# Out-projection of a stream step as three products of high and low parts

## What is computed

```
h   = modulate(x, shift_m, scale_m)                         # adaLN
mix = W_out [ RetentionGroup(h) | StickBreakingGroup(h) ]   # the out-projection, 1024 x 1024
x   = layer_norm(alpha * x + gate_m * mix, ln_mix_g, ln_mix_b)
h   = modulate(x, shift_f, scale_f)
x   = layer_norm(alpha * x + gate_f * HierMoE(h))           # 16 experts, top 2 of one group
```

## Time and profile before

| | us |
|---|---|
| median of 3 launches | 1542.14 |
| lowest, highest | 1540.63, 1542.35 |
| the profiled launch | 1539.93 |
| span of its instructions | 1538.1 |
| mean granted TensorE clock, share of full | 0.947 |

### The profile page before, as it was taken

The page is one execution under the profiler, slowest core; times in us unless marked ns, Lnnn a source line. Parts: engine busy times, 40 slices in busy tenths (PEclk is TensorE's granted clock), DMA queues, the critical chain, the costliest instruction groups (busy, mean ns, idle before and its releaser), DMA issues.

```text
span 1538.1 us, 18365 instructions
## 1 busy us (share of the span) xinstructions
PE 1344.9 (87%) x6487; PEld 890.7 (58%) x6488; DVE 851.6 (55%) x1111; ACT 569.3 (37%) x751; POOL 334.8 (22%) x466
## 2 busy tenths in 40 slices
PE   5989999999899989999979992799999999999900
PEld 1433334466777856656535542588777788787700
DVE  5486875034531056576334556555888551528868
ACT  0200000123222156777422124145777442527632
POOL 0122310000420046676423341100000000000063
PEclk9999999999999999999989995799999999999955
DMA  9614131101121152121312615565899752529863
GB/s 345 242 55 164 55 118 54 55 1 31 38 69 41 49 179 55 29 56 29 138 55 96 246 62 205 194 229 218 311 384 388 281 184 89 218 75 381 315 231 131
DMA packets 138756, 234.44 MB, mean 152 GB/s; under 512 B 57320, under 2 KB 58928, under 8 KB 138696
## 3 DMA queue, kind: packets, MB, share of 16 engines
q1 hardware_dynamic: 128424, 196.39, 36.1%
q0 software_dynamic: 6496, 23.60, 4.5%
q10 hardware_dynamic: 3776, 13.67, 2.2%
HBM read 197.95 MB, written 35.68 MB: 152 GB/s over the span
## 4 chain that ended last, share of the span: by engine, by line
PE 60%; DVE 15%; issue 11%; ACT 5%; POOL 4%; DMA 2%; SPq 1%; ACTq 1%; POOLq 0%; DVEq 0%
PE psum L784 55%; DVE arena L1592 4%; POOL arena L1914 3%; PE psum L967 2%; ACT high L1376 2%; PE psum L1161 1%; DMA arena<-in_w_ada_mix 1%; DVE arena L1855 1%; DVE arena L1854 1%; DVE arena L1847 1%; DVE arena L1845 1%; DVE arena L1846 1%; DVE win_low L1572 1%; DVE arena L1593 1%; ACT a_high L1404 1%
## 5 line engine op out<-in xcount | busy, mean ns | idle before, releaser
L784 PE MATMUL psum<-arena 128*64 128x128 f32 (+7 forms) x1524 | 256.8, 365 | 11.6 <-DVE arena L1785 10.1
L784 PEld LDWEIGHTS psum<-arena 128*64 128x64 f32 (+3 forms) x1524 | 131.3, 157 | 117.2 <-issue 95.9
L784 PE MATMUL psum<-win,hT 128*128 128x512 f32 (+1 forms) x432 | 191.4, 597 | 0.5 <-ACT hT L1205 0.5
L784 PE MATMUL psum<-high,h_high 128*128 128x512 f32 x416 | 165.1, 397 | 2.5 <-DVE h_low L1801 2.5
L784 PE MATMUL psum<-high,h_low 128*128 128x512 f32 x416 | 163.2, 392 | 0.0
L784 PEld LDWEIGHTS psum<-win,hT 128*128 128x128 f32 (+1 forms) x432 | 77.6, 184 | 109.7 <-issue 105.5
L1659 DVE TENSOR_TENSOR_SCAN arena<-arena,psum 128x512 f32<-128x512 f32 (+4 forms) x116 | 109.5, 978 | 19.6 <-ACT arena L1329 19.5
L1796 DVE TENSOR_TENSOR low_odd<-raw_odd,high 128x2048 fp32r<-128x2048 f32 x48 | 107.8, 2289 | 13.9 <-ACT high L1376 13.9
L1796 DVE TENSOR_TENSOR low_even<-raw_even,high 128x2048 fp32r<-128x2048 f32 x48 | 107.7, 2287 | 10.8 <-ACT high L1376 10.8
L1914 POOL TENSOR_TENSOR arena<-arena 128x512 f32<-128x512 f32 (+4 forms) x116 | 108.2, 933 | 9.4 <-POOL arena L1911 0.2
L1958 POOL COPY smalls<-smalls 128x1 int32 x26 | 4.7, 182 | 421.6 <-PE psum L1161 415.9
(11 more groups left out here) (227 smaller groups left out, 2168.0 us busy)
## 6 DMA issues: line engine op xcount, KB each, us to landing
raw_even<-in_w_e_gate SPq DMA_DIRECT2D x8, 2048.0 KB, 10.6
raw_even<-in_w_e_up SPq DMA_DIRECT2D x8, 2048.0 KB, 16.4
raw_even<-in_w_e_down SPq DMA_DIRECT2D x8, 2048.0 KB, 14.7
raw_odd<-in_w_e_gate SPq DMA_DIRECT2D x8, 2048.0 KB, 10.1
raw_odd<-in_w_e_up SPq DMA_DIRECT2D x8, 2048.0 KB, 16.5
raw_odd<-in_w_e_down SPq DMA_DIRECT2D x8, 2048.0 KB, 14.7
win<-in_w_in SPq DMA_DIRECT2D x7, 2048.0 KB, 8.7
expert_rows<-arena ACTq DMA_DIRECT2D x26, 512.0 KB, 6.7
```

Of the source, the lines that this page charges most:

```text
L784: pe_last[0] = nc.tensor.matmul(*x, **y)
```

## The change

`wout` and the mixed input are split into high and low parts, and each product of the out-projection becomes three (`split_products`). The eight chunks of each half of `wout` are split piece by piece (`first_splits`): ACT writes `wout_high` (half 0 into the region of the queries, half 1 into that of the cache), DVE writes `wout_low` in place over `wout`. The first pieces lie in steps NG to NG+4 of the attention, between its last operations. Each tile's mixed rows are split too: ACT writes `mix_high` (128 x 1024, two buffers), DVE writes the low part in place. PE's early products of tile 0 inside the attention go; tile 0 is computed like the others, its first use of each chunk waiting for that piece. In ACT's loop the high part of tile t+1 stands between the two `copy_ret`; in DVE's loop the low part of tile t+1 stands first. `take_scales(*LATE)` moves behind tile 0's second half on DVE, `head_sums(*LATE)` behind half 0 of tile 0 on PE. Since `win_high` and `wout_high` lie where the first expert's weights go, SP issues that load in the last iteration, after all products, ahead of the last tile's stores.

```diff
@@ -198,8 +198,8 @@
 
         projected_f = named([("hT", r_a, KC * TOK), ("win", r_w, 8192)], F32)
-        projected_s = named([("x_low", r_a, KC * TOK), ("win_low", r_w, 8192), ("win_high", r_m, 9 * D),
-                             ("x_high", r_b + 8960, KC * TOK)], F32R)
+        projected_s = named([("mix_high", r_tmp, 2 * KC * P), ("x_low", r_a, KC * TOK), ("win_low", r_w, 8192),
+                             ("win_high", r_m, 9 * D), ("wout_high", r_sq, KC * 512), ("x_high", r_b + 8960, KC * TOK)], F32R)
         cst = view(r_const, C_MAIN)
         rot = view(r_sq, C_END - C_MAIN)
         ident = cst[:, C_IDENT:C_IDENT + 128]
@@ -252,7 +252,7 @@
         mixed = view(r_m, 9, D)
         hT, x_low, x_high = [t[:].rearrange("p (k n) -> p k n", k=KC)
                              for t in (projected_f["hT"], projected_s["x_low"], projected_s["x_high"])]
-        mixT = view(r_a, KC, TOK)
+        mixT = hT
         ada_b = [view(r_b + 4096 * i, KC, 512) for i in range(4)]
         ada_m = [view(r_m + 4096 * i, KC, 512) for i in range(2)]
         ada_rows = view(r_sq + C_END - C_MAIN, 2048)
@@ -262,7 +262,10 @@
         win, win_low = [[t[:, 4096 * i:4096 * i + 4096].rearrange("p (k n) -> p k n", k=KC) for i in range(2)]
                         for t in (projected_f["win"], projected_s["win_low"])]
         win_high = projected_s["win_high"][:].rearrange("p (k n) -> p k n", k=9)[:, 0:KC, 512:1024]
-        wout = view(r_w, KC, D)
+        wout_f = projected_f["win"][:].rearrange("p (k n) -> p k n", k=KC)
+        wout_low = projected_s["win_low"][:].rearrange("p (k n) -> p k n", k=KC)
+        wout_high = [projected_s["wout_high"][:].rearrange("p (k n) -> p k n", k=KC), win_high]
+        mix_high = projected_s["mix_high"][:].rearrange("p (i k q) -> p i k q", i=2, k=KC)
 
         qhT = view(r_b, 4, TOK)
@@ -395,9 +398,10 @@
             for name, table_at in (("cache", cache_at), ("sums", sums_at), ("scales", scales_at)):
                 if s in table_at:
                     enter((name,) + table_at[s], by_dve)
-        enter(("sums",) + LATE, by_dve)
         for t in range(1, TILES):
             enter(("ret", t), by_act, (7,))
+            if t == 1:
+                enter(("sums",) + LATE, by_dve)
             if t == 3:
                 enter(("scales",) + LATE, by_dve)
 
@@ -463,6 +467,23 @@
                         ret_i += 1
         N_TURN = turn_no
         assert N_TURN == 27
+
+        out_split_no = {}
+        for hh in range(2):
+            for k in range(KC):
+                if (hh, k) == (0, 4):
+                    out_split_no["mixed", 0] = len(split_no) + len(out_split_no) + 1
+                out_split_no["wout", hh, k] = len(split_no) + len(out_split_no) + 1
+        for t in range(1, TILES):
+            out_split_no["mixed", t] = len(split_no) + len(out_split_no) + 1
+        first_splits = {NG: [("wout", 0, 0), ("wout", 0, 1), ("wout", 0, 2)],
+                        NG + 1: [("wout", 0, 3), ("mixed", 0), ("wout", 0, 4), ("wout", 0, 5)],
+                        NG + 2: [("wout", 0, 6), ("wout", 0, 7), ("wout", 1, 0)],
+                        NG + 3: [("wout", 1, 1), ("wout", 1, 2), ("wout", 1, 3)],
+                        NG + 4: [("wout", 1, 4), ("wout", 1, 5), ("wout", 1, 6), ("wout", 1, 7)]}
+
+        def tile_cols(t):
+            return slice(t * P, t * P + rows_of(t))
 
         def ada_src(j):
             w = w_ada_mix if j < 6 else w_ada_ffn
@@ -684,7 +705,7 @@
                             "(t p) d -> p t d", p=P)).then_inc(s_kc[1], 16)
 
             load_cache(0)
-            sp.dma_start(wout, w_out[0].rearrange("(k p) n -> p k n", p=P)).then_inc(s_wout, 16)
+            sp.dma_start(wout_f, w_out[0].rearrange("(k p) n -> p k n", p=P)).then_inc(s_wout, 16)
             for pair in range(1, PAIRS):
                 load_cache(pair)
 
@@ -727,11 +748,10 @@
             for t in range(TILES):
                 if t + 2 < TILES:
                     load_x(t + 2)
-                if t == 3:
-                    sp.wait_ge(s_wt, ring_no["ret", LAST])
+                if t == LAST:
+                    sp.wait_ge(s_op, TILES)
                     load_expert(0, 0)
                 store_5(t)
-            sp.wait_ge(s_op, TILES)
             load_expert(1, 1)
             sp.wait_ge(s_lg, 9)
             sp.wait_ge(s_x1o[0], 16 * 5)
@@ -1034,9 +1054,12 @@
 
             def out_part(t, hh, ks):
                 r = rows_of(t)
+                cols = slice(hh * 512, (hh + 1) * 512)
                 for k in ks:
-                    last = mm(psum[t % 2][0:r, hh, :], mixT[:, k, t * P:t * P + r],
-                              wout[:, k, hh * 512:(hh + 1) * 512], start=(k == 0), stop=(k == KC - 1))
+                    if t == 0:
+                        pe.wait_ge(s_pL, out_split_no["wout", hh, k])
+                    last = split_products(psum[t % 2][0:r, hh, :], mix_high[:, t % 2, k, 0:r], x_low[:, k, tile_cols(t)],
+                                          wout_high[hh][:, k, :], wout_low[:, k, cols], k == 0, k == KC - 1)
                 return last
 
             pe.wait_ge(s_mr, 9)
@@ -1057,13 +1080,6 @@
                     head_sums(*sums_at[s])
                 if s in scales_at:
                     head_scales(*scales_at[s])
-                if s == NG + 1:
-                    wait_copied(pe, ("ret", 0))
-                    wait_copied(pe, ("scales", 2, 2))
-                    pe.wait_ge(s_wout, 16)
-                    out_part(0, 0, range(7))
-            out_part(0, 1, range(7))
-            head_sums(*LATE)
 
             def h2_turned(t):
                 r = rows_of(t)
@@ -1088,15 +1104,13 @@
             for t in range(TILES):
                 if t >= 2:
                     pe.wait_ge(s_ope, t - 1)
-                for piece, (t0, _, _) in enumerate(pieces):
-                    if t == t0:
-                        wait_copied(pe, ("scales", PAIRS - 1, piece))
-                if t:
-                    wait_copied(pe, ("ret", t))
+                pe.wait_ge(s_pL, out_split_no["mixed", t])
                 for hh in range(2):
                     if hh == 0 and 2 * t + 1 < TILES:
                         ret_turn(2 * t + 1)
-                    last = out_part(t, hh, range(KC) if t else (7,))
+                    last = out_part(t, hh, range(KC))
+                    if (t, hh) == (0, 0):
+                        head_sums(*LATE)
                     if (t, hh) == (1, 0):
                         head_scales(*LATE)
                     if hh == 0 and 2 * t + 2 < TILES:
@@ -1308,6 +1322,26 @@
                     last = A(mixT[:, k, t * P:t * P + r], bank(7)[:, k * P:k * P + r], ACT.Copy, scale=colv[:, 64 + k:65 + k])
                 last.then_inc(s_wte, 1)
 
+            def out_high(kind, *at):
+
+                if kind == "wout":
+                    hh, k = at
+                    if k == 0:
+                        act.wait_ge(s_wout, 16)
+                        act.wait_ge(s_pv if hh else s_qk, NG)
+                    A(wout_high[hh][:, k, :], wout_f[:, k, hh * 512:(hh + 1) * 512], ACT.Copy).then_inc(s_pH, 1)
+                else:
+                    t, = at
+                    if t >= 2:
+                        act.wait_ge(s_op, t - 1)
+                    else:
+                        act.wait_ge(s_qk, NG)
+                    act.wait_ge(s_wte, by_act["ret", t])
+                    for piece, (t0, t1_, _) in enumerate(pieces):
+                        if t0 <= t < t1_:
+                            wait_copied(act, ("scales", PAIRS - 1, piece))
+                    A(mix_high[:, t % 2, :, 0:rows_of(t)], hT[:, :, tile_cols(t)], ACT.Copy).then_inc(s_pH, 1)
+
             def square(pair, piece):
 
                 cols = piece_cols(piece)
@@ -1336,11 +1370,18 @@
                     copy_ret(0)
                 if s in squares_at:
                     square(*squares_at[s])
+                for split_ in first_splits.get(s, ()):
+                    out_high(*split_)
             square(*LATE)
+            for split_ in first_splits[NG + 4]:
+                out_high(*split_)
             for t in range(TILES + 2):
-                for v in (2 * t + 1, 2 * t + 2):
-                    if v < TILES:
-                        copy_ret(v)
+                if 2 * t + 1 < TILES:
+                    copy_ret(2 * t + 1)
+                if t + 1 < TILES:
+                    out_high("mixed", t + 1)
+                if 2 * t + 2 < TILES:
+                    copy_ret(2 * t + 2)
                 v = t - 1
                 if 0 <= v < TILES:
                     r = rows_of(v)
@@ -1616,6 +1657,18 @@
 
             step(V.tensor_copy(bank(7)[:, 0:1], ones_col))
 
+            def out_low(kind, *at):
+
+                dve.wait_ge(s_pH, out_split_no[(kind,) + at])
+                if kind == "wout":
+                    hh, k = at
+                    cols = slice(hh * 512, (hh + 1) * 512)
```

(15 more changed lines are left out.)

## The result

The changed kernel takes 1528.52 us (median of 4 launches, 1527.12 to 1530.7); the kernel before takes 1541.39 (median of 4). The ratio is 0.9936, 95% interval 0.9917 to 0.9955: faster by 12.9 us. The direction was forecast; the gain is 12.9 us instead of the 27.4 of the sum, and the time lies 0.5 us above the range.

The account below looks back on a forecast made before the run. PE was taken to bound the out-projection stage from tile 3 on. R(8) 25.4 us earlier plus 2.0 in the tail made 27.4 off the profiled 1539.93, as a median 1515 us; range 1506 to 1528.

Parts of the forecast that it names:

- PE's work: Out-projection on PE: 432 float32r products replace 144 float32 ones, so a tile needs 13.6 us instead of 16.4.
- The end of attention: Splits between attention's last operations let PE finish tile 0's products near 774, so R(0) comes 6.6 us earlier.
- R(0): DVE's first read of tile 0, R(t) being that of tile t; forecast 774 instead of 780.64.
- DVE's cycle: DVE's time per tile: 11.35 plus 1.05 more wait for ACT plus 1.23 subtraction, 13.6 us for tiles 4 to 8.
- R(8): DVE's first read of tile 8, on which all later work hangs; forecast 893.9 instead of 919.33, 25.4 us earlier.
- signs of being wrong: Low part waits for ACT beyond one L1363 and one copy; tiles 4 to 8 period above 15; R(8)-to-end grows.
- Tiles 1 to 3: Out-projection tiles with two turns each: PE waits 2 to 3 us before each second turn; 50.9 us in all.
- The charge of 2.3 us for the clock: Added to each of tiles 1 to 3 for PE running slower behind its gap, between 0 and 3.4.
- The tail: After R(8): the last DVE and POOL port collision goes, 2.0 us gained; the later first expert load costs 0.
- the load itself: Rival, chance 0.07: the first expert's weights land 12 to 18 us later, ACT's first use slips 2 to 8; 1517 to 1523.
- The falling clock in every tile: Rival, chance 0.10: PE waits a little in each tile and its clock drops, period 16 to 17; 1529 or 1527.
- Collisions each tile: Rival, chance 0.06: DVE's L1700 meets POOL in every tile, DVE's cycle 15.6 us, R(8) 902.9; 1526.

Follow-up runs that it names:

- e6: Changed kernel with e2's early split and POOL's rstd of tile t between its two h2 operations; ratio 0.9868 to the kernel before.
- e8: Kernel before, float32 products kept, with only take_scales of the last pair moved behind tile 0's second half on DVE; ratio 0.9928.
- e9: Changed kernel with take_scales of the last pair put back ahead of tile 0's read on DVE; ratio 0.9979 to the kernel before.
- e3: Changed kernel with only the high times high product of the three, all splits kept; ratio 0.9907 to the kernel before.
- e1: Changed kernel with POOL's rstd of tile t ahead of the two h2 operations of tile t-1; ratio 0.9891 to the kernel before.
- e10: e6 with ACT's copy_ret of 2t+3 ahead of L1404 of tile t; ratio 0.9760 to the kernel before, 1503.58 us.
- e2: Changed kernel with mixed rows of tile t+2 split before L1404 of tile t on ACT, behind its first statistics on DVE; ratio 0.9925 to the kernel before.
- e5: Changed kernel with the moves of e1 and e2 together; ratio 0.9920 to the kernel before.

## Why the prediction was off

**PE's work: right.** In e6, where PE is the bound, a half of 24 products takes 5.6 us at full clock (836.45 to 842.04), and the period is 13.63.

**The end of attention: right.** R(0) was put at 774 and is 774.34. That take_scales no longer stood before it was named in one sentence, without a price of its own. e8 and e9 show that this clause carried nearly the whole measured gain. So the direction came out right in good part by luck: without that move the change would have been worth 3 us (e9), for the ring and the gaps in tiles 1 to 3 took back most of what the products gave.

**DVE's cycle: the step that failed.** "11.35 + 1.05 + 1.23 = 13.6" kept the 5.63 us from R to L1363 of the trace before. That distance held because DVE waited 5 us for PE ahead of each first read: POOL had begun its two h2 operations meanwhile and was through with them at 855.7, when at 858.7 it was asked for the next rstd. Once DVE no longer waits, they stand in POOL's queue ahead of the rstd: from R to L1404 it is 8.49 us (860.41 to 868.90), the ring 16.33. The prediction even had the place of the pair, 2.6 to 7.4 us behind DVE's last statistics, and used it for port collisions only, not for POOL's own queue. Five steps of 13.6 and one collision, 69.0, became 77.1: 8.1 of the 14.7 us by which the span missed the forecast (1525.4 against 1538.1 - 27.4). The rest is 4.0 in tiles 1 to 3, 0.3 at R(0) and 2.2 behind R(8). e3 shows that PE does not set the period (its work cut, period unchanged), e1 that POOL's order is in it (L1404 back at 5.64, period 16.33 to 15.7), and e6 that with POOL's order and the split's place changed the 13.6 comes. Two of the prediction's own signs of being wrong came: the low part waited 6.41 us for ACT, where the sum had 3.65 (2.60 + 1.05), and the period was above 15.

**Tiles 1 to 3: mechanism right, size off.** Forecast 50.9, measured 54.9. PE's gaps were 1.84, 5.36 and 2.92 instead of 2 to 3, the second long for the same reason: L1404 of tile 1 waits for POOL (797.40, 8.3 after R(1)); with POOL's order changed (e1) it is 2.65. The charge of 2.3 us for the clock was due behind two of the three. e10 shows that these gaps also hang on copy_ret's place on ACT.

**The tail: 2 us expected, none came.** L1760 of tile 8 does take 1.22 us instead of the 3.22 of the earlier trace rows. But POOL's queue gave it back at once: L1404 of tile 8 starts 8.43 us after R(8) instead of 7.56 (926.89 - 919.33). And DVE's wait for the indirect DMA grew to 4.12 us. It is 4.1 to 5.0 in all ten profiles with the late load of the first expert and 1.3 to 1.6 in all four without it, so that load, which is then under way, is the likely cause. L1404 of tile 8 on ACT, and that wait on DVE:

```profile
914.83 1.24 ACT L1404 ACTIVATE arena<-arena,smalls 64x1024 f32<-64x1024 f32 x1 [5.06 <-POOL smalls L618]
```

```profile
929.67 0.91 DVE L1771 MEMSET arena<- 128x1024 f32 x1 [4.12 <-DMA arena<-in_x_prompt,smalls]
```

DVE still waited 0.38 us for PE's logits behind it, so the longer wait cost nothing, as assumed. ACT begins the first expert 31.2 us after R(8), before it was 30.4; the later L1404 is all of that, so the load itself was not late. From R(8) to the end it is 619.0 us against 618.8, and 616.8 forecast. No run moved that load by itself.

**The rivals.** The falling clock in every tile did not come: 1.2 GHz was granted only behind gaps, from tile 4 on in tiles 5 and 7, and e3 shows that PE did not set the period there. Collisions each tile did not come in the changed kernel either: L1760 took 2.61 and 2.52 us in tiles 2 and 3, but from tile 4 on the ring keeps DVE and POOL apart. They did come in e1, e2, e5 and e6 as soon as the ring was shortened. A ring through POOL was not among the rivals.

## What to carry to other kernels

When the engine that bounds a stage gets faster, redraw the order of the work on every other engine's queue without the waits that the slow engine gave them: what was done in a wait now stands ahead of something. Check it on the chip by cutting the supposed bound's work to a third; if the period stays, look for a ring of latencies, and try the order of two instructions in it before making any engine faster. And when a change carries a small move along, run the move alone on the old kernel: here it was worth as much as the whole change, and only with three such orders set right did the products pay their 18 us.

## What was not expected of the hardware

A 0.57 us POOL instruction on one column per partition took 1.61 us beside DVE's subtraction of 1024 columns with two SBUF inputs (e2, both beginning near 836.0, the subtraction ending at 837.24): in this collision the small instruction paid the rest of the large one's length. And the length of a gap of PE does not tell by itself whether the clock falls behind it. Gaps of 1.84 us (changed kernel, granted clock 1.00 behind it) and 2.88 us (e6) between dense halves left it up. Gaps of 1.61 us ahead of the small products in the earlier trace rows, of 1.08 us ahead of them in the changed kernel, and of 2.43 us between dense halves in e8 did not. What decides between them no run here shows.
